# A hybrid decoder block on one core: head pairs requested in the attention, front loads reordered, first gate operands split early, last stage inside the expert block

## What is computed

```python
mod = jax.nn.silu(c) @ w_ada[l] + b_ada[l]                    # six rows of 1024
sh_m, sc_m, gt_m, sh_f, sc_f, gt_f = jnp.split(mod, 6, axis=-1)
h = modulate(rmsnorm(x, g_norm_mix[l]), sh_m, sc_m)
z = h @ w_in[l]
z_rwkv, z_mla, z_gates = jnp.split(z, [RWKV_COLS, RWKV_COLS + MLA_COLS], axis=-1)
y_rwkv = rwkv7_branch(z_rwkv, ...)                            # a recurrence over the tokens, 8 heads
y_mla = mla_branch(z_mla, ...)                                # causal attention, 8 heads
gate_rwkv, gate_mla = jnp.split(jax.nn.sigmoid(z_gates), 2, axis=-1)
merged = gate_rwkv * (y_rwkv @ w_branch[l, 0]) + gate_mla * (y_mla @ w_branch[l, 1])
x = x + gt_m[:, None, :] * (merged @ w_out[l])
h2 = modulate(rmsnorm(x, g_norm_ffn[l]), sh_f, sc_f)
x = x + gt_f[:, None, :] * hier_moe(h2, ...)                  # 32 experts, two per token
```

## Time and profile before

| | |
|---|---|
| median of 3 runs | 1646.56 us (1640.95 to 1651.13) |
| the profiled execution | 1642.19 us, span of its trace 1640.4 us |
| PE busy | 1406.6 us, 86% |
| DVE / ACT / POOL busy | 704.8 / 465.3 / 263.9 us |
| front, to the first barrier | 0 to 336 us |
| stages 2 and 3 | 336 to 624.7 us |
| stage 4 | 624.7 to 684.4 us |
| attention | 684.4 to 855.1 us |
| gates to experts | 855.1 to 1605.4 us |
| last stage | 1605.4 to 1640.4 us |

### The profile page before, as it was taken

One profiled execution on the slowest core, in us unless ns is written; L12 is line 12 of the kernel. 1 busy time (PEld: TensorE's weight loads), 2 busy tenths in 40 slices (PEclk: granted clock), 3 DMA queues, 4 the chain that ended last, 5 costly groups with the idle time before them and its releaser, 6 DMA issues. The chain is left out here.

```text
span 1640.4 us, 32997 instructions
## 1 busy us (share of the span) xinstructions
PE 1406.6 (86%) x14393; PEld 1012.2 (62%) x14393; DVE 704.8 (43%) x991; ACT 465.3 (28%) x828; POOL 263.9 (16%) x302
## 2 busy tenths in 40 slices
PE   4699999947999994599979999999895699999980
PEld 0587777716999993377768888787784333333320
DVE  0745686656666536344443111355335321212114
ACT  1543233243334433244443222212211111111110
POOL 0201222106555630011110000000000111111110
PEclk8899999977999997799999999999997699999995
DMA  9831222200000007910011111314106689999947
GB/s 356 283 120 52 84 78 71 77 15 2 4 4 4 4 4 267 289 48 1 1 48 43 51 48 41 143 49 158 39 39 271 263 320 414 414 419 408 393 170 307
DMA packets 78759, 238.08 MB, mean 145 GB/s; under 512 B 8472, under 2 KB 41752, under 8 KB 61984
## 3 DMA queue, kind: packets, MB, share of 16 engines
q1 hardware_dynamic: 71280, 219.30, 36.4%
q0 software_dynamic: 7344, 16.79, 2.7%
HBM read 209.82 MB, written 36.19 MB: 150 GB/s over the span
## 5 line engine op out<-in xcount | busy, mean ns | idle before, releaser
L2430 PE MATMUL ps<-gu,xT 128*32 128x512 f32 x1536 | 175.9, 599 | 1.7 <-DMA gu<-w_e_up 1.0
L339 PE MATMUL ps<-hs,wh 128*128 128x512 f32 x320 | 126.7, 396 | 11.4 <-DVE hs L335 7.7
L341 PE MATMUL ps<-hs,wl 128*128 128x512 f32 x320 | 126.3, 395 | 0.0
L2430 PEld LDWEIGHTS ps<-gu,xT 128*32 128x32 f32 x1536 | 47.8, 111 | 106.5 <-issue 102.6
L2642 DVE TENSOR_TENSOR sg<-sg,ps 128x256 f32<-128x256 f32 x25 | 10.5, 421 | 211.3 <-ACT sg L2516 211.3
L340 PE MATMUL ps<-hs,wh 128*128 128x512 f32 x256 | 100.1, 391 | 0.0
L335 DVE TENSOR_TENSOR wl<-wraw,wh 128x1024 fp32r<-128x1024 f32 x24 | 29.4, 1225 | 156.1 <-ACT wh L332 156.1
L339 PE MATMUL ps<-hh,wr_h 128*128 128x512 f32 x224 | 93.2, 416 | 0.5 <-DVE wr_l L335 0.5
L1879 DVE TENSOR_REDUCE nmax<-ps 128x1 f32<-128x896 f32 (+4 forms) x64 | 45.9, 753 | 99.6 <-PE ps L1790 99.0
L340 PE MATMUL ps<-hl,wr_h 128*128 128x512 f32 x224 | 88.5, 395 | 0.0
L341 PE MATMUL ps<-hh,wr_l 128*128 128x512 f32 x224 | 88.5, 395 | 0.0
(11 more groups left out here) (364 smaller groups left out, 3012.2 us busy)
## 6 DMA issues: line engine op xcount, KB each, us to landing
gu<-w_e_gate SPq DMA_DIRECT2D x34, 1024.0 KB, 12.9
gu<-w_e_up SPq DMA_DIRECT2D x34, 1024.0 KB, 15.3
dn<-w_e_down SPq DMA_DIRECT2D x34, 1024.0 KB, 11.5
wbuf<-w_ada SPq DMA_DIRECT2D x16, 1024.0 KB, 13.7
wbuf<-w_ada SPq DMA_DIRECT2D x16, 512.0 KB, 5.2
wraw<-w_gates SPq DMA_DIRECT2D x16, 512.0 KB, 3.3
rows<-expert_rows SPq DMA_DIRECT2D x16, 512.0 KB, 10.3
wr<-w_rwkv SPq DMA_DIRECT2D x14, 512.0 KB, 3.8
```

The source lines that it names most:

```text
L339: nc.tensor.matmul(out, wt[0], mov[0], start=(k == 0), stop=False)
L341: return nc.tensor.matmul(out, wt[1], mov[0], start=False, stop=(k == kn - 1))
L2430: last = nc.tensor.matmul(ps[part, GB[b]], xT[:, b, k, part], gu[:, expert(m, c_) % WB, :, k], start=(k == 0), stop=(k == KD - 1))
```

## The change

Four edits.

**Front.** SP issues the eight `w_ada` loads ahead of the four x tiles (they alternated), and the constants after the fifth of them (they came first). The four matmuls that spread the shift and scale rows over the partitions run with scale first, and DVE copies scale out after two of them. The low part of `wm` moves from POOL to DVE, after tile 1.

**Head pairs.** `load_pair` is called for pair 0 in stage 4 as before; pairs 1 to 3 are issued at the start of the attention, ahead of gate weights and h.

**First gate operands.** In units 24 to 30 of the attention ACT makes one high part each (gate weights 0 and 1, then row blocks 3 to 7 of h; 1024 columns each) at the end of the unit's work, and DVE the low part. The next stage makes blocks 0 to 2 only, one by one, and PE's gate tiles take the blocks in the order 3 to 7, 0 to 2.

**Last stage.** It is written into the block of the experts: ACT, when all indirect stores have landed, increments `all_out`, SP waits for that and issues the loads. The stage's own `phase()` is gone, and with it one barrier pair; its three semaphores join those of the experts, so that 73 are cleared in one go after the output.

```diff
@@ front
                     sp.dma_start(ccol[:], c[0].rearrange("(p k) -> p k", k=KD)).then_inc(c_in, 16)
-                    sp.dma_start(cst[:], consts).then_inc(const_in, 16)
...
                     for k in range(KD):
                         rows0.load(sp, k)
-                        if k % 2:
-                            load_x(k // 2)
+                        if k == CH:
+                            sp.dma_start(cst[:], consts).then_inc(const_in, 16)
+                    for t in range(4):
+                        load_x(t)
...
-                    pool.wait_ge(wm_hi, 1)
-                    nc.gpsimd.tensor_tensor(wm_l[:], wm[:], wm_h[:].bitcast(f32), ALU.subtract).then_inc(wm_lo, 1)
...
-                    act.wait_ge(bc_mm, 1)
+                    act.wait_ge(bc_mm, CH)
...
-                    dve.wait_ge(bc_mm, 1)
+                    dve.wait_ge(bc_mm, 2)
                     link(nc.vector.tensor_copy(SC_M, ps[:, 2:4].rearrange("p a n -> p (a n)")))
...
+                            if t == 1:
+                                dve.wait_ge(wm_hi, 1)
+                                low_part(wm_l[:], wm[:], wm_h[:]).then_inc(wm_lo, 1)
...
-                    for j in range(CH):
-                        m = nc.tensor.matmul(ps[:, j], sel[:, j], row0, start=True, stop=True)
-                    m.then_inc(bc_mm, 1)
+                    for j in (2, 3, 0, 1):
+                        nc.tensor.matmul(ps[:, j], sel[:, j], row0, start=True, stop=True).then_inc(bc_mm, 1)
@@ stage 4
-                    pair(0)
+                    load_pair(sp, 0)
                     for k in range(KD):
                         rows2.load(sp, k)
-                    for p in range(1, HEADS // 2):
-                        pair(p)
@@ attention
+        KLATE = 3
+        SPLITS = [None, None] + list(range(KLATE, KD))
+        SPLIT_AT = 24
...
                     def _(sp):
+                        for p in range(1, HEADS // 2):
+                            load_pair(sp, p)
                         gate_weights(sp, 0, 0)
...
+                        def split_high(n):
+                            k = SPLITS[n]
+                            if k is None:
+                                act.wait_ge(w_in7[n], 16)
+                                high_part(wh[:, n], wraw[:, n]).then_inc(split_hi, 1)
+                            else:
+                                act.wait_ge(y_out4, 32)
+                                act.wait_ge(mod_out, 16 * 2 * CH)
+                                act.wait_ge(h_in7[k // PIECE], 16)
+                                high_part(hh[:, k], hraw[:, 1, k]).then_inc(split_hi, 1)
...
                             if u + 1 < NU:
                                 exponentials(u + 1)
+                            if 0 <= u - SPLIT_AT < len(SPLITS):
+                                split_high(u - SPLIT_AT)
...
+                        def split_low(n):
+                            k = SPLITS[n]
+                            dve.wait_ge(split_hi, n + 1)
+                            if k is None:
+                                low_part(wl[:, n], wraw[:, n], wh[:, n]).then_inc(split_lo, 1)
+                            else:
+                                low_part(hl[:, k], hraw[:, 1, k], hh[:, k]).then_inc(split_lo, 1)
@@ gates
                 def gate_tile(i, br, first):
-                    pe.wait_ge(w_lo, 2 * i + (br + 1))
                     if not first:
+                        pe.wait_ge(w_lo, 2 * i + (br - 1))
                         pe.wait_ge(g_ev, 2 * i + (br - 1))
-                    for k in range(KD):
-                        if first and br == 0 and k % PIECE == 0:
-                            pe.wait_ge(h_lo, k // PIECE + 1)
+                    for j, k in enumerate([*range(KLATE, KD), *range(KLATE)]):
+                        if first and br == 0 and k < KLATE:
+                            pe.wait_ge(h_lo, k + 1)
...
-                weights(0, 16)
-                for j in range(KD // PIECE):
-                    rows = slice(PIECE * j, PIECE * (j + 1))
-                    act.wait_ge(h_in[j], 16)
-                    high_part(hh[:, rows], hraw[:, 1, rows]).then_inc(h_hi, 1)
-                    if j == 1:
-                        weights(1, 16)
+                for k in range(KLATE):
+                    high_part(hh[:, k], hraw[:, 1, k]).then_inc(h_hi, 1)
@@ last stage, now in the experts' block
-                for b in range(1, YSLOTS):
-                    pool.wait_ge(y_out[b], 16 * (FIXED // YSLOTS))
-                pool.sem_inc(stored, 1)
...
                 act.wait_ge(y_out[0], n * 16 + 16 * (FIXED // YSLOTS))
                 act.sem_inc(turned, 1)
+                for b in range(1, YSLOTS):
+                    act.wait_ge(y_out[b], 16 * (FIXED // YSLOTS))
+                act.sem_inc(all_out, 1)
...
+            @block.sync
+            def _(sp):
+                sp.wait_ge(all_out, 1)
+                for t in range(NT):
+                    for i in range(2):
+                        at = i * SEQ + t * P
+                        sp.dma_start(rows[:, 2 * t + i], y_dram[at:at + P]).then_inc(r_in[2 * t + i], 16)
+                for t in range(NT):
+                    sp.wait_ge(acc, 2 * t + 2)
+                    sp.dma_start(out_v[t], x1[:, t]).then_inc(o_out, 16)
+                sp.wait_ge(o_out, 16 * NT)
...
-        with phase() as st:
-            rows = sb(st, "rows", [P, 2 * NT, D])
```

More of the change, by code:

```diff
@@ L2147, in weights @@
                     low_part(wl[:, b], wraw[:, b], wh[:, b]).then_inc(w_lo, 1)
-                weights(0, 1)
-                for j in range(KD // PIECE):
-                    rows = slice(PIECE * j, PIECE * (j + 1))
-                    dve.wait_ge(h_hi, j + 1)
-                    low_part(hl[:, rows], hraw[:, 1, rows], hh[:, rows]).then_inc(h_lo, 1)
-                    if j == 1:
-                        weights(1, 2)
+                for k in range(KLATE):
+                    dve.wait_ge(h_hi, k + 1)
+                    low_part(hl[:, k], hraw[:, 1, k], hh[:, k]).then_inc(h_lo, 1)
                 dve.wait_ge(y_hi, 1)
@@ L2186, in _ @@
                         merge(i, b)
-                        weights(b, 2 * i + (b + N_GATES + 3))
+                        weights(b, 2 * i + (b + N_GATES + 1))
                         merged(2 * i + b)
@@ L2244, in build @@
             dn = sb(st, "dn", [P, WB, 2, D])
+            rows = alias("rows", [P, 2 * NT, D], f32)
             gu = sb(st, "gu", [P, WB, 2, KD, FE])
@@ new lines, in build, with _ @@
+            out_v = out[0].rearrange("(t p) d -> t p d", p=P)
+            @block.vector
+            def _(dve):
+                for t in range(NT):
+                    for i in range(2):
+                        dve.wait_ge(r_in[2 * t + i], 16)
+                        if i:
+                            dve.wait_ge(acc, 2 * t + 1)
+                        nc.vector.scalar_tensor_tensor(x1[:, t], rows[:, 2 * t + i], top[:, i, t:t + 1], x1[:, t],
+                                                       ALU.mult, ALU.add).then_inc(acc, 1)
```

68 lines of the change are left out of this document (25 added, 43 removed).

## The result

The changed kernel takes 1628.55 us (median of 4 runs, 1625.34 to 1630.19), the kernel before 1647.65 us beside it (1640.95 to 1651.13): a ratio of 0.989 with a 95% interval of 0.985 to 0.992. In a second comparison with more executions it was 1627.99 us (1623.18 to 1630.28) against 1649.92 us, 0.986 (0.984 to 0.988). So the change makes the kernel 19 to 22 us faster; 1623 us had been forecast, with 21.8 us of gain.

The account below looks back on a forecast made before the run. PE, busy 86% of the span, bounds the kernel; only its idle stretches can shrink. 0.2 + 3.2 + 12.9 - 3.5 + 6.0 + 3.0 = 21.8 us gives 1620.4 from the profile or 1624.8 from the median; forecast 1623, range 1612 to 1634.

Parts of the forecast that it names:

- Loads reordered, 0: Front: the last x tile has the same bytes ahead of it and lands at 33.3 again; worth 0.
- Scale first 0.2: Front: DVE's scale copy starts earlier, so the first `hb` waits only for ACT's copy; 0.2 us gained.
- `wm_l` 3.2: Front: moving `wm_l` to DVE ends the hold-up by POOL, PE gets tile 2 earlier; 3.2 us, ends 0.3 and 4.
- from there to the end of the front PE has no wait of size, so the gain is kept: Front after the first `mla`: no sizeable PE wait follows, so the 3.2 us gain lasts.
- Rival C: Front gives 0.3 because tile 0's store holds ACT and PE, end 2, gates 5; gain 15.8, 1629 us; chance 0.08.
- Head pairs 12.9: End of stage 4: SP ends at 669.3 instead of 682.24, so attention starts 12.9 us earlier; bounds 11 and 14.
- Rival E: Stage 4: `w_ada` loads, not pairs, fill SP's queue, taking half of 12.9; gain 15.3, 1630 us; chance 0.05.
- Splits -3.5: Attention: seven splits delay maxima by 2.6 us, plus 0.9 for a clock fall; costs 3.5 us, bounds 0 and 8.4.
- Rival B: Attention pays about 11.8 instead of 3.5 through clock falls, POOL contention and DVE's order; gain 13.5, 1631 us; chance 0.12.
- rival D: Attention: added PE wait leaves the clock at half until its end, 41 us lost; 19 slower, about 1661 us; chance 0.03.
- Start of the gates 6.0: Gates: PE starts with the barrier, 5.3 us earlier, and its clock may hold; 6.0 us, ends 5.0 and 7.0.
- Last stage 3.0: End: loads start 7.8 us earlier, but 4.5 us of clears only move behind the output; 3.0 us, ends 2 and 4.

Follow-up runs that it names:

- e1_pairs: Kernel before with one part only: head pairs 1 to 3 requested at the start of the attention instead of in stage 4; 1636.32 us against 1648.73, ratio 0.991.
- e5_after: The changed kernel again without an edit, with more executions and a second profile; 1627.99 us, ratio 0.986 to the kernel before.
- e7_lag: Changed kernel with ACT's high parts in the attention one unit earlier than DVE's low parts; 1625.04 us, ratio 0.985 to the kernel before.
- e10_best: Changed kernel with high parts one unit earlier, mod rows stored in the attention, no final clearing, recurrence's 38 semaphores kept; 1613.70 us, ratio 0.980 to the kernel before.
- e9_mod: Changed kernel with the four mod row stores issued at the attention's start, not at stage 4's end; 1624.20 us, ratio 0.986 to the kernel before.

## Why the prediction was right, and where its sizes were off

The sum of 21.8 us was made against the profiled execution of before. Its own terms, with what the table gives as the mean of the kernels without a part less the mean of those with it:

**Loads reordered, 0.** PE's scale products start no earlier. The reason held: the last x tile has the same bytes ahead of it. What the term left out is PE's longer idle time ahead of these products; by itself the reorder made the kernel before 2.8 us slower, for a reason that stays open (e12_loads). In the whole change such a loss would be inside the front's 2.9 us below.

**Scale first 0.2 and `wm_l` 3.2.** Scale first gave 0.1 us: the first `hb` starts 1.14 us behind the start of ACT's copy, 1.26 before. The low part of tile 0 took 1.22 us, PE had tile 2 3.6 us earlier (forecast 3.3) and the first `mla` matmul at 60.08 (forecast 60.4). At the recurrence the means differ by 2.9 us (373.1 of five, 370.2 of nine), but the two first profiles differ by 0.1 us only. Where the 3.6 us went in the profile after, PE's timeline at tile 4 shows:

```profile
73.94 1.09 PE L809 MATMUL ps<-cst,YTM 128*128 128x128 f32 x8 [1.83 <-DVE YTM L664]
74.97 1.85 PE L317 MATMUL ps<-wbuf,crep 128*32 128x256 f32 x16
76.75 0.72 PE L339 MATMUL ps<-wm_h,hh 128*128 128x416 f32 x1
77.26 0.55 PE L340 MATMUL ps<-wm_l,hh 128*128 128x416 f32 x1
```

A PE wait of 1.83 us was followed by a stretch at 1.2 GHz (the row products took 1.07 us, the matmuls 0.35, in the profile of before), 1.6 us lost, and a second such stretch at the norm products behind 342.70 took 1.4 us. The step that failed is "from there to the end of the front PE has no wait of size, so the gain is kept": a wait of 1.64 us at tile 4 was in the trace of before, and behind the same wait the clock fell in five of the nine profiles with the new front. So the term came out near its 3.4 us as a mean, 2.9, and what the first profile kept of it, 0.1 us, is one draw. Rival C's mechanism, the store that holds ACT, is real; it shows in the old front, when the addition of tile 1 is the operation held (PE's wait at tile 4 is 3.83 us in e1_pairs), and not in the new one, where ACT waits as long (3.74 us) and PE does not wait for it.

**Head pairs 12.9.** 11.9 us (18.2 less 6.3). What was mis-sized is the end of SP's work: four rows at 1.53 us in the earlier trace rows took 2.92 here. SP ended 3.6 us behind the start of line 324 instead of the 2.2 that the forecast's 669.3 means, and PE started 2.66 us behind SP's end, as before (2.75). The trace of before could not show what those issues take once the queue is free. Rival E fell with e1_pairs.

**Splits -3.5.** To PE's first gate matmul the five kernels with the splits as in the change take 172.9 us on the mean, and 170.1 had been the time to the barrier: -2.8 us. It is -2.0 in three profiles and -4.0 in two, and the difference is the fall of the clock. I had put it in with half of 1.7 us; where it came it was 6.8 us long, twice what I had taken, and cost about 2. The two PE waits grew as said: the one for DVE's results from 1.4 to 2.3 us (forecast 2.5), and one of 1.75 us for the exponentials came up in e5_after. That DVE's waits for ACT, and not the low parts, are the price, my working had in its numbers (the low part starts when ACT's high part ends) and not in its words; the runs showed that it can be had for nothing.

The low parts took 1.22 to 1.23 us each, but none of them ran beside an operation of POOL in any of the five profiles, so the changed kernel does not test what it costs when they do. e7_lag does. There five of the seven ran beside one, and its timeline has these:

```profile
801.09 1.38 DVE L335 TENSOR_TENSOR hs<-hraw,hs 128x1024 fp32r<-128x1024 f32 x1
...
806.81 1.22 DVE L335 TENSOR_TENSOR hs<-hraw,hs 128x1024 fp32r<-128x1024 f32 x1
806.89 1.47 POOL L1845 TENSOR_TENSOR YTM<-ob 128x128 f32<-128x128 f32 x1
```

DVE's low part took at most 1.38 us, and the POOL operation that started behind it 1.47 instead of 0.46; PE's waits did not grow. The Trainium skill (GPSIMD Engine Reference, Key points) has it that POOL and VectorE contend when the VectorE instruction has two SBUF inputs. These rows agree with it, as does the front, where DVE's operation took 8.12 us beside POOL's 7.88; in each of them the held operation lost no more than what was left of the other's, and in the attention that was short. Rival B did not come (2.0 to 4.0 us and not 11.8), nor did rival D: the longest stretch at 1.2 GHz behind such a wait was 6.8 us.

**Start of the gates 6.0.** PE starts 0.0 us behind the barrier instead of 5.3, and the gates are 1.0 us shorter (297.0 less 296.0): 6.3.

**Last stage 3.0.** 3.1 us (350.4 less 347.3): the loads 7.8 us earlier, the clears moved behind the last store, as worked out.

**The sum.** 2.9 + 11.9 - 2.8 + 6.3 + 3.1 = 21.4 us. The recurrence and stage 4, which no part touches up to line 324, take 1.2 us more in the kernels with the pairs' part (298.1 against 296.9 on the mean, e10_best left out; it builds up in steps of under 1 us, and the two groups overlap, 297.0 to 299.0 and 296.6 to 297.2). No run tells whether that is the change or scatter; it stays open. With it the sum is 20.2, between the 19.1 and 21.9 us of the two comparisons.

**The base.** That 1623 was 5 us under the result is this step: "the median of the runs shown is 4.4 us higher ... I take 1623, near the middle". The profiled execution of before was one of the quick ones in its front (370.45 us; 373.1 is the mean of five), a part that the change makes steadier. The median of 28 runs was 1648.73, and 1646.56 less 21.8, 1624.8, would have been the number that the sum supports; 1648.7 less 21.8 is 1626.9.

**Two slips in the rivals.** Rival C adds 12 us for the head pairs where the term says 12.9; with it C's gain is 16.7 us and its time 1628. Rival D's 1661 stands on the profiled execution, 1642.2, while B, C and E stand on 1623 plus 21.8; on that base it is 1664. Neither bears on the forecast.

## What to carry to other kernels

If one engine's share of a split work hangs on another's, put the two a unit apart in their orders: the wait costs, not the work. The profiled execution is one draw; a sum of gains belongs on the median of many runs, and where two engines race for a start within a microsecond the trace shows one outcome only, so ask what each of the two starts hangs on. Ask of each queue at a barrier which of its issues must stand ahead of it, and of each clearing whether anything uses the semaphore again.

## What the runs showed of the hardware that I had not expected

- Which operation of DVE is held by a long one of POOL is decided by 1 us: the low part of tile 0 (7.78 us in the earlier trace rows) or the addition of tile 1 (8.12 us in e1_pairs). An addition that had started 0.36 us ahead of POOL's operation took its 1.23 us; the next with two SBUF inputs was held, and ended 1.1 us behind POOL's end. In five profiles of five the outcome followed the length of PE's products ahead of it, 5.2 to 5.4 us or 6.0 to 6.4.
- Beside a short POOL operation the same kind of DVE operation lost at most 0.16 us, and a POOL operation that started behind it took 1.47 us instead of 0.46 (e7_lag).
- The same PE wait of 2.3 us was followed by 6.8 us at 1.2 GHz in two profiles and by none in three. So the price of a wait of this size is a chance, here about 2 us or nothing.
- SP's issue of the same four rows took 1.17 us at the start of the attention (e9_mod), and at the end of stage 4 1.53 us in the profile of before and 2.92 in that of the changed kernel. No run tells why.
